# The last stage of a decoder step: output features turned on VectorE and put in token order through DRAM

## The reference

```python
x = x + f                                   # f: the down projection of the feed-forward
...
y_prompt = rms_norm(xp[:, N_META:], final_g)
y_sample = rms_norm(xs, final_g)

def rms_norm(x, g):
    xf = x.astype(jnp.float32)
    out = xf * lax.rsqrt(jnp.mean(xf * xf, axis=-1, keepdims=True) + EPS)
    return (out * g.astype(jnp.float32)).astype(x.dtype)
```

## Time and profile before

| | us |
|---|---|
| median of 3 runs | 1065.07 (1064.83 to 1065.54) |
| the profiled execution, device time | 1064.65 |
| its span | 1062.9 |
| TensorE busy | 1051.9 (99% of the span) |
| VectorE busy | 636.7 (60%) |
| ScalarE busy | 388.5 (37%) |
| GpSimd busy | 371.6 (35%) |

### The profile page before, as it was taken

One profiled execution on the slowest core, in us unless ns is written; L12 is line 12 of the kernel. 1 busy time (PEld: TensorE's weight loads), 2 busy tenths in 40 slices (PEclk: granted clock), 3 DMA queues, 4 the chain that ended last, 5 costly groups with the idle time before them and its releaser, 6 DMA issues.

```text
span 1062.9 us, 19390 instructions
## 1 busy us (share of the span) xinstructions
PE 1051.9 (99%) x7944; PEld 1027.5 (97%) x7944; DVE 636.7 (60%) x971; ACT 388.5 (37%) x562; POOL 371.6 (35%) x180
## 2 busy tenths in 40 slices
PE   8999999999999999999999999999999999999997
PEld 7999999999999999999999999999999999999997
DVE  6777457954543464362643339999940189999413
ACT  6566787313332334232422343222211122222332
POOL 4333344333222222232123434344433344334430
PEclk9999999999999999999999999999999999999999
DMA  7443322336378594783442233222323222233312
GB/s 196 160 110 92 103 74 80 85 105 163 86 216 213 131 266 118 187 247 90 149 171 82 80 100 99 80 80 80 102 81 96 60 80 80 82 95 97 97 44 89
DMA packets 234656, 123.46 MB, mean 116 GB/s; under 512 B 57387, under 2 KB 230427, under 8 KB 234318
## 3 DMA queue, kind: packets, MB, share of 16 engines
q1 hardware_dynamic: 234364, 122.20, 41.4%
q10 hardware_dynamic: 210, 0.07, 0.0%
HBM read 99.31 MB, written 20.73 MB: 113 GB/s over the span
## 4 chain that ended last, share of the span: by engine, by line
PE 98%; ACT 1%; POOL 1%; issue 0%; DVE 0%; POOLq 0%; DVEq 0%
PE ring L2106 48%; PE ring L2526 23%; PE bank L2526 17%; PE bank L2396 2%; PE bank L2383 1%; PE bank L2153 1%; PE bank L2364 1%; PE bank L2376 1%; PE bank L2438 1%; PE bank L2263 1%; PE bank L2426 1%; POOL x_split L940 0%; PE bank L2127 0%; PE bank L2572 0%; ACT sq_tok L1023 0%; PE bank L2296 0%
## 5 line engine op out<-in xcount | busy, mean ns | idle before, releaser
L2106 PE MATMUL ring<-x_split,whi 128*128 128x256 f32 (+1 forms) x2016 | 358.8, 300 | 0.0
L928 POOL TENSOR_TENSOR wlo<-stage,whi 128x1024 fp32r<-128x1024 f32 x78 | 194.5, 2494 | 408.2 <-ACT whi L986 408.2
L2106 PEld LDWEIGHTS ring<-x_split,whi 128*128 128x128 f32 x2016 | 304.2, 189 | 8.1 <-issue 7.6
L2106 PE MATMUL ring<-x_split,wlo 128*128 128x256 f32 (+1 forms) x1008 | 217.5, 297 | 0.0
L2106 PEld LDWEIGHTS ring<-x_split,wlo 128*128 128x128 f32 x1008 | 169.9, 189 | 0.0
L986 ACT ACTIVATE whi<-stage 128x1024 fp32r<-128x1024 f32 x80 | 84.3, 1054 | 96.4 <-PE ring L2106 81.6
L971 POOL TENSOR_TENSOR wlo<-stage,whi 128x1024 fp32r<-128x1024 f32 x28 | 71.9, 2568 | 108.0 <-ACT whi L1341 108.0
L2526 PE MATMUL ring<-x_split,whi 128*128 128x256 f32 (+1 forms) x512 | 88.7, 295 | 0.0
L1457 DVE SCALAR_TENSOR_TENSOR conv<-up,cols,conv 128x592 f32<-128x592 f32 x88 | 75.5, 858 | 3.1
L2526 PEld LDWEIGHTS ring<-x_split,whi 128*128 128x128 f32 x512 | 77.0, 189 | 0.0
L2012 DVE TENSOR_SCALAR conv<-up,cols 128x592 f32<-128x592 f32 x44 | 72.2, 1641 | 3.1
(11 more groups left out here) (368 smaller groups left out, 2066.5 us busy)
## 6 DMA issues: line engine op xcount, KB each, us to landing
stage<-in_w_in SPq DMA_DIRECT2D x56, 512.0 KB, 4.1
stage<-in_w_up SPq DMA_DIRECT2D x44, 512.0 KB, 3.8
stage<-in_w_down SPq DMA_DIRECT2D x16, 704.0 KB, 4.4
stage<-in_w_branch_a SPq DMA_DIRECT2D x8, 512.0 KB, 3.7
c_sample<-in_state_mlstm_C SPq DMA_DIRECT2D x16, 256.0 KB, 6.9
out_s_mlstm_C<-c_sample SPq DMA_DIRECT2D x16, 256.0 KB, 2.4
stage<-in_w_branch_b SPq DMA_DIRECT2D x8, 512.0 KB, 3.8
stage<-in_w_out SPq DMA_DIRECT2D x8, 512.0 KB, 3.8
```

Of the source, the lines that this page charges most:

```text
L928: pool.tensor_tensor(spaced(wlo[:, slot]), packed(stage[:, slot, 0:n]), spaced(whi[:, slot]).bitcast(F32), ALU.subtract).then_inc(w_lo, 1)
L2106: last = pe.matmul(of(z, t0 or -2, t1), w[:, kk * WS:kk * WS + P], x_, start=kk == 0 and m == 0, stop=kk == kn - 1 and m == 2)
```

## The change

Six of the eight feature blocks leave the TensorE turns. In the loop over the tiles of the down projection, VectorE turns feature block m-1, already gained, in 32x32 blocks into one of three buffers `y_blocks`, for m = 1 to 6 (`dve.transpose`). SyncE writes each with four DMAs (`store_feature`) to a DRAM tensor `out_rows` of 576 rows, in runs of 32 floats. Blocks 0 and 1 are written behind the last load of `w_down` and ahead of the stores of the convolution's state, blocks 2 to 5 behind them. When all six are in DRAM, two DMAs read features 0 to 767 back into `y`, now with tokens on the partitions (`y_in`). Features 768 to 1023 (blocks 6 and 7) are turned by TensorE as before.

Token tiles are counted from the first prompt token now, so that all of them begin on a row of the output: tiles 0 to 3 have 128 rows each, tile 4 the 64 sample tokens. Each tile is scaled by one engine, in two instructions: 768 features in place in SBUF, 256 out of PSUM. VectorE has tiles 0, 2 and 4, ScalarE tiles 1 and 3. Five DMAs store y in place of six.

```diff
+        y_blocks = [sb(f"y_blocks{n}", [P, TD], ...) for n in range(3)]
...
+                    def store_feature(m):
+                        sp.wait_ge(y_turned, m + 1)
+                        for a_ in range(4):
+                            d0 = P * m + 32 * a_
+                            sp.dma_start(ydram.rearrange("(b t) d -> t b d", t=32)[:, :, d0:d0 + 32],
+                                         y_blocks[m % 3][32 * a_:32 * a_ + 32, :].rearrange("p (b f) -> p b f", f=32)
+                                         ).then_inc(y_stored[m % 3], 16)
+                    store_feature(0)
+                    store_feature(1)
                     sp.wait_ge(fc_evicted, 1)
                     for j in range(FC_SET):
                         fc_store(j)
+                    for m in range(2, 6):
+                        store_feature(m)
+                    for n in range(3):
+                        sp.wait_ge(y_stored[n], 16 * 4 * 2)
+                    sp.dma_start(y[:, 0:TT - 1, 0:6 * P], ydram[0:SEQ, 0:6 * P].rearrange("(i p) d -> p i d", p=P)
+                                 ).then_inc(y_in, 16)
+                    sp.dma_start(y[0:TD - SEQ, TT - 1, 0:6 * P], ydram[SEQ:TD, 0:6 * P]).then_inc(y_in, 16)
...
             for i in range(TT):
-                sp.wait_ge(y_act, i + 1)
-                sp.wait_ge(y_dve, i + 1)
-                if i == 0:
-                    sp.dma_start(yp[0:P - META], y[META:P, 0]).then_inc(y_out, 16)
-                elif i < TT - 1:
-                    sp.dma_start(yp[P * i - META:P * i - META + P], y[:, i]).then_inc(y_out, 16)
+                if i % 2:
+                    sp.wait_ge(y_act, i + 1)
                 else:
-                    sp.dma_start(yp[SEQ - TAIL:SEQ], y[0:TAIL, i]).then_inc(y_out, 16)
-                    sp.dma_start(ys, y[TAIL:LAST, i]).then_inc(y_out, 16)
+                    sp.wait_ge(y_dve, i + 2)
+                if i < TT - 1:
+                    sp.dma_start(yp[P * i:P * i + P], y[:, i]).then_inc(y_out, 16)
+                else:
+                    sp.dma_start(ys, y[0:TD - SEQ, i]).then_inc(y_out, 16)
...  ScalarE
+            def scaled(i):
+                act.activation(y[:, i, 0:6 * P], y[:, i, 0:6 * P], ACT.Copy, scale=rmsf[:, i:i + 1]).then_inc(y_act, 1)
+            def turned_scaled(i):
+                act.wait_ge(fin_turned, i + 1)
+                act.activation(y[:, i, 6 * P:D], final(i), ACT.Copy, scale=rmsf[:, i:i + 1]).then_inc(y_act, 1)
             root(0)
+            act.wait_ge(fin_rms, 1)
+            act.wait_ge(y_in, 32)
+            scaled(1)
+            root(1)
+            turned_scaled(1)
+            act.wait_ge(fin_rms, 2)
+            scaled(3)
+            turned_scaled(3)
...  VectorE, in the loop over the tiles m of the down projection
                     if h and m >= 2:
                         accumulate(m - 1)
+                    if h and m:
+                        dve.wait_ge(fin_gain, m)
+                        if m > 3:
+                            dve.wait_ge(y_stored[(m - 1) % 3], 16 * 4)
+                        dve.transpose(y_blocks[(m - 1) % 3][:, :], resid[:, m - 1, META:]).then_inc(y_turned, 1)
...  VectorE, at the end
+            def scaled(i):
+                n = P if i < TT - 1 else TD - SEQ
+                dve.wait_ge(fin_rms, 1 if i < 2 else 2)
+                ts(y[0:n, i, 0:6 * P], y[0:n, i, 0:6 * P], rmsf[0:n, i:i + 1], None, ALU.mult).then_inc(y_dve, 1)
+                dve.wait_ge(fin_turned, i + 1)
+                ts(y[0:n, i, 6 * P:D], final(i)[0:n], rmsf[0:n, i:i + 1], None, ALU.mult).then_inc(y_dve, 1)
             inverse(0)
+            dve.wait_ge(y_in, 32)
+            scaled(0)
+            inverse(1)
+            scaled(2)
+            scaled(4)
...  TensorE
             sums(facc, range(2), stop=False)
             pe.wait_ge(fin_gain, 7)
             pe.wait_ge(fc_evicted, 1)
-            turns(0, range(7))
+            for i in range(4):
+                turn_out(i, 6)
             pe.wait_ge(fin_sq, 8)
             sums(fsq[2], range(2), start=False).then_inc(fin_sum, 1)
             pe.wait_ge(fin_last, 1)
-            turns(0, [7]).then_inc(fin_turned, 1)
-            turns(1, range(8)).then_inc(fin_turned, 1)
+            turn_out(0, 7).then_inc(fin_turned, 1)
+            turn_out(1, 7).then_inc(fin_turned, 1)
             pe.wait_ge(fin_acc, 7)
             sums(facc, range(2, TT)).then_inc(fin_sum, 1)
             pe.wait_ge(fin_first, 2)
             pe.wait_ge(fin_last, 2)
-            turns(2, range(8)).then_inc(fin_turned, 1)
-            pe.wait_ge(fin_root, 2)
-            turns(3, range(8)).then_inc(fin_turned, 1)
-            pe.wait_ge(y_act, 1)
-            pe.wait_ge(y_dve, 1)
-            turns(4, range(8)).then_inc(fin_turned, 1)
+            turn_out(2, 7).then_inc(fin_turned, 1)
+            turn_out(3, 7).then_inc(fin_turned, 1)
+            turn_out(4, 6)
+            turn_out(4, 7).then_inc(fin_turned, 1)
```

More of the change, by code:

```diff
@@ L408, in ffn_weight @@
             return whi[:, s], wlo[:, s]
-        y = sb("y", [P, TT, D], o_h)
-        fsq = [sb("fin_sum", [P, TW], o_a), sb("fin_sq0", [P, TW], o_a + 4 * TW), sb("fin_sq1", [P, TW], o_a + 8 * TW)]
-        facc, f7 = fsq[0], sb("fin_last", [P, TW], o_a + 12 * TW)
+        FIN = META + TW
+        fsq = [sb("fin_sum", [P, FIN], o_a), sb("fin_sq0", [P, FIN], o_a + 4 * FIN), sb("fin_sq1", [P, FIN], o_a + 8 * FIN)]
+        facc, f7 = fsq[0], sb("fin_last", [P, FIN], o_a + 12 * FIN)
+        y = sb("y", [P, TT, D], o_a + 16 * FIN)
+        y_blocks = [sb(f"y_blocks{n}", [P, TD], o_a + 16 * FIN + 4 * D * TT + 4 * TD * n) for n in range(3)]
+        assert 16 * FIN + 4 * D * TT + 12 * TD <= 16 * TB + LINE
         cols = sb("cols", [P, NROW * P], o_p)
@@ L440, in hybrid_layer @@
         kdram, vdram = (nc.dram_tensor(n_, [TW, DH], F32, kind="Internal").ap() for n_ in ("key_rows", "value_rows"))
+        ydram = nc.dram_tensor("out_rows", [TD, D], F32, kind="Internal").ap()
         edram = nc.dram_tensor("inter_rows", [HEADS, T], F32, kind="Internal").ap()
@@ L497, in hybrid_layer, with final @@
         late_ring = [wide[(T_FFN + m) % 2] for m in range(2)]
-        final = [bank2(0), bank2(1), late_ring[1], late_ring[0], bank2(0)]
+        def final(i):
+            return bank[:, i, 0:2 * P] if i < 4 else late_ring[1][:, 0:2 * P]
         fsum = late_ring[0][:, 0:2], late_ring[0][:, 512:512 + TT - 2]
-        CUT = 2 * P
+        CUT = META + 2 * P
         w_loaded = [sem("w_loaded0"), sem("w_loaded1")]
@@ L553, in hybrid_layer @@
         y_act, y_dve = sem("y_act"), sem("y_dve")
+        y_turned, y_in = sem("y_turned"), sem("y_in")
+        y_stored = [sem(f"y_stored{n}") for n in range(3)]
         y_out = sem("y_out")
@@ L875, in _ @@
                         fc_store(j)
+                    for m in range(2, 6):
[5 more added lines that the diff above has]
+                    sp.dma_start(y[0:TD - SEQ, TT - 1, 0:6 * P], ydram[SEQ:TD, 0:6 * P]).then_inc(y_in, 16)
             yp, ys = o["y_prompt"][0], o["y_sample"].rearrange("b l d -> (b l) d")
             for i in range(TT):
[L879 to L887 removed]
+                if i % 2:
+                    sp.wait_ge(y_act, i + 1)
+                else:
+                    sp.wait_ge(y_dve, i + 2)
[3 more added lines that the diff above has]
+                    sp.dma_start(ys, y[0:TD - SEQ, i]).then_inc(y_out, 16)
             for s, n in ((lru_out, 4), (m_out, 2), (cp_out, 4), (n_out, 2), (f_out, 2 * FC_SET),
[L889 removed]
+                         (y_out, TT)):
                 sp.wait_ge(s, 16 * n)
@@ L1439, in root @@
                 act.activation(rmsf[:, i0:i1], fsum[n], ACT.Sqrt, scale=1.0 / D, bias=eps).then_inc(fin_root, 1)
-            root(0)
[L1441 to L1448, removed]
+            def scaled(i):
[3 more added lines that the diff above has]
+                act.activation(y[:, i, 6 * P:D], final(i), ACT.Copy, scale=rmsf[:, i:i + 1]).then_inc(y_act, 1)
+            root(0)
+            act.wait_ge(fin_rms, 1)
[6 more added lines that the diff above has]
+            turned_scaled(3)
         @block.vector
@@ L2059, in _ @@
                             st(dve.memset(b_[:, 0:META], 0.0))
-                            st(dve.memset(b_[:, T:TW], 0.0))
+                            st(dve.memset(b_[:, T:FIN], 0.0))
                         st.wait()
@@ L2079, in inverse @@
                 dve.reciprocal(rmsf[:, i0:i1], rmsf[:, i0:i1]).then_inc(fin_rms, 1)
-            inverse(0)
[L2081 to L2087, removed]
+            def scaled(i):
[4 more added lines that the diff above has]
+                ts(y[0:n, i, 6 * P:D], final(i)[0:n], rmsf[0:n, i:i + 1], None, ALU.mult).then_inc(y_dve, 1)
+            inverse(0)
+            dve.wait_ge(y_in, 32)
[3 more added lines that the diff above has]
+            scaled(4)
         @block.tensor
@@ L2562, in sums, with turn_out @@
```

(11 more changed lines are left out.)

## The result

The changed kernel takes 1068.11 us (median of 8 runs, 1067.62 to 1069.0), the kernel before 1064.90 us in the same comparison (8 runs, 1064.6 to 1065.75). The ratio is 1.0031, 95% interval 1.0022 to 1.0039: slower by 0.31%, 3.2 us. The time lies in the range given. The likeliest case, 1066.95 and "no change that can be told", missed by 1.2 us and lost to the case of a slower kernel, which had a chance of 0.38.

A forecast was written before the change was run, and what follows sets the result against it. The end was taken as bound by one y transfer starting with the first store. First store +2.85 and stream -0.95 gave span +1.9, 1064.8; adding 1.75 and 0.42 gave 1066.95 us, range 1065.3 to 1069.0.

The forecast's parts named there:

- likeliest case: Whole kernel: span +1.9 us to 1064.8, time 1066.95 us, +0.18%, just inside what a measurement can tell; chance 0.53.
- the case of a slower kernel: Whole kernel: slower than before by more than 0.2% (2.1 us); chance 0.38.
- what sets the end: End of kernel: one transfer of 2.36 MB from the first y store on; TensorE finishing 2.4 us earlier is worth 0.
- Rival C: End of kernel: the way through DRAM is hidden, y_in before 1053.3, total 1064.4 us, no change to tell; chance 0.03.
- the parts beside the product: Last down projection: six VectorE turns of some 0.74 us, state's stores moved 4.3 us to 1022.2; cost 0.
- The step that failed: the read back: After the last block store: 1728 KB from DRAM, issued 1048.9, 6.9 us to y_in at 1055.8; bounds 5.9 and 8.1.
- the block stores: SyncE's queue, block 5: last of four stores issued at 1046.4, landing 2.5 us later at 1048.9; bounds 1048.6 and 1050.8.
- Rival B: Block stores land late, 3.9 instead of 2.5 us with longer issues: up to +1.9 us, 1068.85; chance 0.10.
- The stream of y stores: First y store to end of span: 7.8 us instead of 8.75, so -0.95 us.
- the slow last piece: End of the y stores: 250 GB/s blamed on a small DMA's 1.15 us issue; 0.7 us taken as gained.
- Rival A: Read back, one DMA with nothing else queued, at 273 GB/s: 8.1 us instead of 6.9, total 1068.15; chance 0.30.
- first scaling to first store: Tile 0 on VectorE: can be stored 1.2 us after y_in, against 0.83 us behind the first scaling before.

The follow-up runs named there:

- second look: The changed kernel with 96 waits on a long satisfied semaphore added to TensorE's program, in feed-forward tiles 1 to 12: 1067.75 us, ratio 1.0027.

## Why the prediction was right or wrong

**Right: what sets the end.** The end is one transfer that starts with the first tile, and TensorE's turns are beside it. Taking the read back off the path gave the time of the kernel before three times over (ratios 0.9998, 0.9997, 0.9996), with TensorE done 2.5 to 3 us earlier. Rival C, which I had priced at "no change" for this reason, is what these runs are.

**Right: the parts beside the product.** Six turns of 0.77 us (0.74 expected), the last from 1043.88 to 1044.65; tile 7 evicted where it was; the state's stores moved to 1024.3 instead of 1022.2, since the first eight block stores took 7.0 us beside a load where I had counted 4.3, and nobody waited.

**Too long: the block stores.** The last was issued at 1046.14 and landed 2.0 us later, where I took 2.5 from the stores of 640 columns. The read back was issued at 1048.20, 0.7 us early. Rival B did not come.

**The step that failed: the read back.** I gave it 6.9 us from the first issue to y_in, with 8.1 as the upper bound; it took 8.9 (1048.20 to 1057.10). Up to 1.3 us of the 2.0 are one packet that my sum did not have. TensorE's program is fetched in packets of 16 KB (the page counts 63 of them, 1.03 MB, for 15828 matmuls and weight loads), one about every 16.6 us, and the last five of each run took 0.9 to 1.4 us, each on one DMA engine. The one at the end fell into the read back. One engine then came last, and everybody waited for it. Moving the packet by 7 to 9 dummy turns took 1.3 us off the changed kernel's 8.9 and 0.7 off the 8.3 of its second look. The other 0.7 us remain with the packet out of the way (7.6 us). I put them down to two things, which no run takes apart: the second read back is issued 0.4 us behind the first and lands that much later, which I had not counted, and the first 1.2 us moved 97 to 105 GB/s where I had put 188.

**The stream of y stores** took 8.13 us instead of 7.8. I had counted the slow last piece as gained because it was due to a late issue. It was due to its 64 rows and is still there: 232 GB/s, 0.9 us. What gain there is came from the first tile, which I had read as slow because it was alone. Reading 273 GB/s as the price of a lone transfer was wrong; its shape was the reason (378 GB/s at the same place with the aligned tiles), and the read back, alone in the queues, ran at 411 once it was going.

**Rival A gave 1068.15, the run 1068.11, and that is chance.** Its place was right, the read back, but its mechanism, a lone transfer at 273 GB/s, did not happen: the main part ran at 411. Put together: -0.7 (block stores) + 2.0 (read back) - 0.15 (first scaling to first store, 1.04 instead of 1.2) + 0.35 (stream) is +1.5 us on the span, 1066.3 instead of 1064.8. The chances were drawn from a read back that could be some 1 us longer; it was 2.0 longer, outside its own bounds, and the block stores, 0.7 us early, kept the total from the upper end of the range.

**What stays open.** That the late engine is the one that carried the packet is inferred: an engine came last by itself in the three kernels with the packet in the read back's data and in none of the four with dummies; the profile does not name the engines. The packet lasts 0.94 us in the changed kernel, and the last engine was some 1.5 us behind; moving the packet won 0.7 to 1.3 us. Whether it costs more than its own length stays open with two executions on one side and two on the other. Nor did I try whether the packet always comes by the same DMA engine.

## What to carry to other kernels

When a result is sent through DRAM to get another layout, read back each part as soon as it is there; what hangs on the last wait should be the last part alone (288 KB landed in 2.6 us here, 1728 KB in 8.9). Work taken off an engine at the end is worth nothing while a stream of stores that hardly pauses sets the end: look at the DMA share behind the last instruction before pricing such a change. A large transfer that someone waits for ends with its slowest engine, so look in the trace for what else uses the DMA engines in that stretch.

## What the runs showed of the hardware that I had not expected

- A 16 KB packet of TensorE's program goes over one of the sixteen DMA engines of the core and took 0.9 to 1.4 us; in a read back that is waited for it cost 0.7 to 1.3 us, among four 72 KB stores 0.7 us (issues 2.70 instead of 1.98) or 1.5 us (landing 3.5 instead of 2.0).
- Waits on satisfied semaphores did not move these fetches and did not add to the count of instructions; dummy matmuls did.
- Stores of whole 4 KB rows ran at 378 to 407 GB/s with 128 rows, 273 with 112 rows from partition 16 on, and 197 to 249 in the stretches with the 64-row piece, with the DMA engines busy at 94% to 112% in all of them.
- Reads of 2.5 and 3 KB rows moved 92 to 105 GB/s in their first 1.0 to 1.2 us of data, then some 400.
